# The last layer norm of a decoder step: bias and scaling moved from VectorE to TensorE and PSUM

## The reference, cut to what matters

```python
def layer_norm(x, g, b):
    mu = jnp.mean(xf, axis=-1, keepdims=True)
    var = jnp.mean(jnp.square(xf - mu), axis=-1, keepdims=True)
    y = (xf - mu) * lax.rsqrt(var + LN_EPS)
    return (y * g + b).astype(x.dtype)
...
x = layer_norm(ALPHA * x + moe_ffn(x, router_w, router_b, w_gate, w_up, w_down), ln2_g, ln2_b)
```

## Time and profile before

| | us |
|---|---|
| median of three executions | 1706.83 |
| the profiled execution, its whole time | 1705.88 |
| its span, first to last instruction | 1704.1 |
| TensorE busy | 1597.7 (94%) |
| VectorE busy | 687.1 (40%) |
| ScalarE busy | 382.9 (22%) |
| GpSimd busy | 43.4 (3%) |

### The profile page before, as it was taken

One profiled execution on the slowest core, in us unless ns is written; L12 is line 12 of the kernel. 1 busy time (PEld: TensorE's weight loads), 2 busy tenths in 40 slices (PEclk: granted clock), 3 DMA queues, 4 the chain that ended last, 5 costly groups with the idle time before them and its releaser, 6 DMA issues.

```text
span 1704.1 us, 23703 instructions
## 1 busy us (share of the span) xinstructions
PE 1597.7 (94%) x10374; PEld 1076.3 (63%) x10374; DVE 687.1 (40%) x991; ACT 382.9 (22%) x396; POOL 43.4 (3%) x79
## 2 busy tenths in 40 slices
PE   8999999999999999999999999898998988988995
PEld 8999999988999999983433432433334324324432
DVE  6546678647467565654620120200201101202706
ACT  5453555523344333240000000000000000000000
POOL 2000000012000000000000000000000000000000
PEclk9999999999999999999999999999999999999998
DMA  8675565579646759978999999999999999999996
GB/s 239 183 223 155 143 186 161 149 210 321 174 137 186 222 179 272 322 272 355 406 390 429 428 428 429 428 428 429 428 428 428 429 428 428 428 429 428 427 417 228
DMA packets 252719, 545.86 MB, mean 320 GB/s; under 512 B 6080, under 2 KB 219152, under 8 KB 228320
## 3 DMA queue, kind: packets, MB, share of 16 engines
q1 hardware_dynamic: 245888, 527.06, 82.0%
q0 software_dynamic: 4640, 15.47, 2.8%
q10 hardware_dynamic: 2112, 2.16, 0.4%
HBM read 537.73 MB, written 6.95 MB: 320 GB/s over the span
## 4 chain that ended last, share of the span: by engine, by line
PE 81%; DMA 13%; DVE 3%; ACT 2%; issue 1%; DVEq 0%; POOL 0%; ACTq 0%
PE bank L890 18%; PE bank L955 13%; PE bank L607 12%; PE bank L608 12%; PE bank L609 12%; DMA ring_high<-wu 9%; PE bank L865 5%; PE bank L1011 3%; PE bank L650 2%; DMA ring_high<-wd 2%; DMA ring_low<-w_in 1%; PE bank L976 1%; PE bank L945 1%; DMA ring_low<-wob 1%; ACT xt L1185 1%
## 5 line engine op out<-in xcount | busy, mean ns | idle before, releaser
L609 PE MATMUL bank<-x_hi,w_lo 128*128 128x264 f32 x1216 | 344.9, 284 | 0.0
L607 PE MATMUL bank<-x_hi,w_hi 128*128 128x264 f32 x1200 | 344.1, 287 | 0.0
L608 PE MATMUL bank<-x_lo,w_hi 128*128 128x264 f32 x1200 | 340.7, 284 | 0.0
L1226 DVE TENSOR_TENSOR w_lo<-ring_low,w_hi 128x2048 fp32r<-128x2048 f32 x107 | 245.1, 2291 | 146.6 <-ACT w_hi L1058 145.8
L890 PE MATMUL bank<-ring_low,reg_pk 128*64 128x512 f32 x1008 | 224.7, 595 | 21.1 <-DMA ring_low<-wu 18.6
L1058 ACT CAST w_hi<-ring_low 128x2048 fp32r<-128x2048 f32 x107 | 203.5, 1902 | 157.3 <-PE bank L609 90.0
L890 PE MATMUL bank<-ring_high,reg_pk 128*64 128x512 f32 x1024 | 225.1, 593 | 7.2 <-DMA ring_high<-wu 6.8
L609 PEld LDWEIGHTS bank<-x_hi,w_lo 128*128 128x128 f32 x1216 | 228.7, 188 | 0.0
L607 PEld LDWEIGHTS bank<-x_hi,w_hi 128*128 128x128 f32 x1200 | 226.8, 189 | 0.9 <-issue 0.8
L608 PEld LDWEIGHTS bank<-x_lo,w_hi 128*128 128x128 f32 x1200 | 227.0, 189 | 0.0
L890 PEld LDWEIGHTS bank<-ring_low,reg_pk 128*64 128x64 f32 x1008 | 69.7, 137 | 171.0 <-issue 132.1
(11 more groups left out here) (339 smaller groups left out, 1769.7 us busy)
## 6 DMA issues: line engine op xcount, KB each, us to landing
ring_low<-w_in SPq DMA_DIRECT2D x76, 1024.0 KB, 5.8
ring_high<-wg SPq DMA_DIRECT2D x34, 2048.0 KB, 23.8
ring_low<-wu SPq DMA_DIRECT2D x33, 2048.0 KB, 25.6
ring_high<-wd SPq DMA_DIRECT2D x32, 2048.0 KB, 27.5
ring_low<-wd SPq DMA_DIRECT2D x31, 2048.0 KB, 18.4
ring_low<-wg SPq DMA_DIRECT2D x30, 2048.0 KB, 33.6
ring_high<-wu SPq DMA_DIRECT2D x30, 2048.0 KB, 23.5
ring_low<-wo SPq DMA_DIRECT2D x16, 1024.0 KB, 6.5
```

What stands on the lines that cost most here:

```text
L607: pe.matmul(out, hi[k], of_hi[:, k, :], start=(k == 0), stop=False)
L608: pe.matmul(out, hi[k], of_lo[:, k, :], start=False, stop=False)
L609: mm = pe.matmul(out, lo[k], of_hi[:, k, :], start=False, stop=(k == kk - 1))
L1226: dve.tensor_tensor(lo_of(q), raw_of(q), hi_of(q).bitcast(F32), ALU.subtract).then_inc(lo_ready, 1)
```

## The change

- The two 1 MB broadcasts of gain and bias (`ln2p`) are gone. GpSimd loads instead 8 rows of 512 values (`ln2_rows`), a gain row and a bias row on partitions 32c and 32c + 1 for each column block.
- TensorE broadcasts the gain rows by four products (`gain_out`), placed in `down_last` behind the products of block 0. ScalarE copies the four banks to `ln2_gain` in SBUF.
- In `down_last` the scatter of block `c` - 1 moves from behind the products of block `c` to their middle, behind row group 3. The last unit is loaded in two halves, and TensorE waits for the second half before row group 4.
- Behind the last prompt add, TensorE broadcasts the bias rows into seven banks (`row_out`), the eighth when bank 0 has been read.
- For each piece VectorE runs only `centred`. TensorE multiplies the piece by a diagonal matrix of one over the standard deviation (`spread`) and accumulates onto the bias in PSUM (`y_part`). ScalarE makes the two diagonals and copies each bank out to `acc`, and SyncE writes it to the output.
- VectorE norms the sample tokens after the prompt pieces. ScalarE starts their four output transfers. TensorE's two small products for them stand behind pieces 3 and 5.

The diff, without the declarations and the overflow branch:

```diff
@@ sync
+                        if m < UNITS - 1:
+                            sp.dma_start(by_block(ring_slot(s)), src).then_inc(landed[s], 16)
+                        else:
+                            sp.dma_start(by_block(ring_slot(s))[:, 0:4, :], src[:, 0:4, :]).then_inc(landed[s], 16)
+                            sp.dma_start(by_block(ring_slot(s))[:, 4:8, :], src[:, 4:8, :]).then_inc(half_in, 16)
...
-            for a, par in enumerate((ln2g, ln2b)):
-                sp.dma_start(ln2p[:, a, :], par.partition_broadcast(P)).then_inc(ln2_in, 16)
...
+            for n in range(8):
+                tt, c = divmod(n, 4)
+                sp.wait_ge(y_ready, n + 1)
+                sp.dma_start(y[P * tt:P * tt + P, 512 * c:512 * c + 512], acc[:, tt, 512 * c:512 * c + 512]).then_inc(y_out, 16)
@@ gpsimd
+            pool.wait_ge(hid_ready, 2 * NPAIR - 1)
+            for c in range(4):
+                for a, par in enumerate((ln2g, ln2b)):
+                    pool.dma_start(ln2_rows[32 * c + a:32 * c + a + 1, :], par[512 * c:512 * c + 512].unsqueeze(0)).then_inc(rows_in, 16)
@@ tensor
+            def row_out(bank, c, a):
+                rows = slice(32 * c, 32 * c + 2)
+                return pe.matmul(bank[:, :], ident[rows, 32 * c + a:32 * c + a + 1].broadcast_to([2, P]), ln2_rows[rows, :], start=True, stop=(a == 0))
+            def gain_out():
+                for c in range(4):
+                    mm = row_out(psum[c], c, 0)
+                return mm
@@ down_last
                     for k in range(8):
+                        if c == 3 and k == 4:
+                            pe.wait_ge(half_in, 16)
                         for half in range(2):
                             mm = pe.matmul(...)
+                        if c and k == 3:
+                            scatter_last(i, c - 1)
                     mm.then_inc(w_used, 1)
-                    if c:
-                        scatter_last(i, c - 1)
+                    if c == 0:
+                        pe.wait_ge(rows_in, 16 * 8)
+                        gain_out().then_inc(gain_mm, 1)
@@ end of tensor
+            pe.wait_ge(gain_ev, 4)
+            pe.wait_ge(sc_ev, pairs * N_SC + (NPAIR * N_SC - 1))
+            for c in range(4):
+                row_out(psum[c], c, 1)
+            for c in range(3):
+                row_out(psum[5 + c], c, 1)
+            def y_part(n):
+                tt, c = divmod(n, 4)
+                bank = psum[n if n < 4 else n + 1 if n < 7 else 0]
+                if n == 0:
+                    pe.wait_ge(spread_ready, 1)
+                if n == 7:
+                    pe.wait_ge(y_ready, 1)
+                    row_out(bank, 3, 1)
+                pe.wait_ge(y_mul, n + 1)
+                pe.matmul(bank[:, :], spread[:, tt, :], acc[:, tt, 512 * c:512 * c + 512], start=False, stop=True).then_inc(y_mm, 1)
...
+            for n in range(4):
+                y_part(n)
+            sample_average(0)
+            for n in range(4, 6):
+                y_part(n)
+            sample_average(1)
+            for n in range(6, 8):
+                y_part(n)
@@ scalar
+                            if c == 0:
+                                act.wait_ge(gain_mm, 1)
+                                for q in range(4):
+                                    act.copy(ln2_gain[:, 512 * q:512 * q + 512], psum[q][:, :]).then_inc(gain_ev, 1)
...
+            act.wait_ge(l_inv, 2)
+            for tt in range(2):
+                ins = act.activation(spread[:, tt, :], ident[:, :], ACT.Identity, scale=mv[:, tt, 3:4])
+            ins.then_inc(spread_ready, 1)
...
+            for n in range(6):
+                y_done(n)
             act.wait_ge(l_var, 4)
             act.activation(mv[:, 2, 2:3], mv[:, 2, 1:2], ACT.Sqrt, bias=eps).then_inc(l_std, 1)
+            for n in range(6, 8):
+                y_done(n)
+            act.wait_ge(ys_ready, 1)
+            for nn in range(4):
+                act.dma_start(y[2 * P:2 * P + NS, 512 * nn:512 * nn + 512], acc_s[32 * nn:32 * nn + NS, :]).then_inc(y_out, 16)
@@ vector
             for tt in range(2):
                 dve.bn_aggr(mv[:, tt, 0:2], stat[:, tt, 0:4, :].rearrange("p n s -> p (n s)")).then_inc(l_var, 1)
+            dve.wait_ge(gain_ev, 4)
+            centred(0)
+            dve.wait_ge(l_std, 2)
+            dve.reciprocal(mv[:, 0:2, 3], mv[:, 0:2, 2]).then_inc(l_inv, 1)
+            centred(1)
             link(dve.bn_stats(stat[:, 2, 0, :], acc_s))
             dve.bn_aggr(ms[:, 0:2], stat[:, 2, 0, :]).then_inc(s_part, 1)
...
+            centred(2)
+            centred(3)
+            centred(4)
             dve.wait_ge(s_part, 1)
             dve.wait_ge(s_avg, 1)
...
             dve.tensor_tensor(ms[:, 1:2], ms[:, 1:2], ms[:, 2:3], ALU.add).then_inc(s_part, 1)
+            centred(5)
             dve.wait_ge(s_avg, 2)
             dve.tensor_copy(ms[:, 0:1], psum[4][:, 0:1])
             dve.tensor_copy(ms[:, 1:2], psum[4][:, 1:2]).then_inc(l_var, 1)
+            centred(6)
             dve.wait_ge(l_std, 3)
             link(dve.reciprocal(ms[:, 3:4], ms[:, 2:3]))
+            centred(7)
             dve.wait_ge(ln2q_in, 16 * 8)
...
```

More of the change, by code:

```diff
@@ L235, in build @@
         xg = reg_pk[:, 0:KD * P].rearrange("p (k s) -> p k s", s=P)
-        ln2p = low[:, 2, :].rearrange("p (a c) -> p a c", c=D)
+        ln2_gain = low[:, 2, 0:D]
+        ln2_rows = reg_pk[:, KD * P:KD * P + 512]
         ln2q = low[:, 3, 0:1024].rearrange("p (a c) -> p a c", c=512)
@@ L287, in build @@
         pick, _ = place("pick", [P, 3, 2, CAP])
+        spread = pick[:, 0:2, :, :].rearrange("p a b s -> p (a b s)").rearrange("p (t q) -> p t q", q=P)
         outer = pick[:, 0:2, :, :].rearrange("p a b s -> p (a b s)")
@@ L454, in _ @@
             with sp.If(pairs > 0):
+                sp.wait_ge(gain_ev, 4)
                 with sp.Fori(0, pairs) as j:
@@ L1035, in _, with sample_average @@
                     pair(j + NPAIR)
-            pe.wait_ge(quarter_ready, 1)
-            for n in range(2):
-                pe.wait_ge(s_part, n + 1)
-                pe.matmul(psum[n][:, 0:1], quarter, mv[:, 2, n:n + 1], start=True, stop=True).then_inc(s_avg, 1)
+                pe.wait_ge(sc_ev, pairs * N_SC + NPAIR * N_SC)
+                gain_out().then_inc(gain_mm2, 1)
+                pe.wait_ge(gain_ev2, 4)
+            pe.wait_ge(gain_ev, 4)
[14 more added lines that the diff above has]
+                pe.matmul(bank[:, :], spread[:, tt, :], acc[:, tt, 512 * c:512 * c + 512], start=False, stop=True).then_inc(y_mm, 1)
+            def sample_average(n):
+                pe.wait_ge(s_part, n + 1)
+                pe.matmul(psum[4][:, n:n + 1], quarter, mv[:, 2, n:n + 1], start=True, stop=True).then_inc(s_avg, 1)
+            pe.wait_ge(quarter_ready, 1)
+            for n in range(4):
[6 more added lines that the diff above has]
+                y_part(n)
         @block.scalar
@@ L1715, in _ @@
                 dve.wait_ge(again, 1)
+                dve.wait_ge(gain_ev2, 4)
             ms = mv[:, 2, :]
@@ L1719, in _, with centred @@
                 dve.bn_aggr(mv[:, tt, 0:2], stat[:, tt, 0:4, :].rearrange("p n s -> p (n s)")).then_inc(l_var, 1)
+            dve.wait_ge(gain_ev, 4)
+            def centred(n):
+                tt, c = divmod(n, 4)
+                cols = slice(512 * c, 512 * c + 512)
+                dve.scalar_tensor_tensor(out=acc[:, tt, cols], in0=acc[:, tt, cols], scalar=mv[:, tt, 0:1], in1=ln2_gain[:, cols],
+                                         op0=ALU.subtract, op1=ALU.mult).then_inc(y_mul, 1)
+            dve.wait_ge(l_var, 3)
+            centred(0)
+            dve.wait_ge(l_std, 2)
+            dve.reciprocal(mv[:, 0:2, 3], mv[:, 0:2, 2]).then_inc(l_inv, 1)
+            centred(1)
             dve.wait_ge(sc_ev, pairs * N_SC + NPAIR * N_SC)
@@ L1763, in _ @@
             dve.scalar_tensor_tensor(out=acc_s, in0=acc_s, scalar=ms[:, 3:4], in1=ln2q[:, 1, :], op0=ALU.mult, op1=ALU.add).then_inc(ys_ready, 1)
-            for n in range(5, 8):
-                centred(n)
-                scaled(n - 1)
-            scaled(7)
 def kernel(**inputs):
```

48 lines of the change are left out of this document (12 added, 36 removed).

## The result

The changed kernel took 1712.21 us in the median of six runs (1709.74 to 1715.35), the kernel before 1706.80 (1705.02 to 1708.11). The ratio is 1.0038 with a 95% interval of 1.0023 to 1.0053, so 3.9 to 9.0 us slower. The forecast was 1712.0. The time is right; of the terms it was made of, the one for the gain rows was 2.5 us too high and the one for the layer norm 1.4 us too low.

A forecast was written before the change was run, and what follows sets the result against it. The end was taken as TensorE until block 3 is scattered, then VectorE's adds, then the layer norm. Terms +2.7 + 1.2 + 0 + 1.5 = +5.4 us gave 1712.2 on the median, stated as 1712.0, range 1708.3 to 1714.8.

The forecast's parts named there:

- part 1: Gain rows in down_last: four row products, 3.44 us behind block 0, make everything behind later, +2.7 us (+2.5 to +3.1).
- part 2: Scatter in the block's middle: VectorE adds block c - 1 only after block c, +1.2 us (0 to +1.93).
- part 3: Split load of the last unit and missing broadcasts: 0, since TensorE reaches block 3 after the whole unit landed.
- part 4: Layer norm shared with TensorE: 18.6 us from L1719 to the end, before 17.1, so +1.5 us.
- the prediction's own signs: Wrong if row products pace under 0.7 us, block 1 starts before 1666, or pieces are late for VectorE, not TensorE.
- the third rival: TensorE's clock falls to 1.2 GHz in the layer norm through gaps of 1.0 and 0.4 us: about +13, 1725; chance 0.03.
- the second rival: Gain and bias rows of 2 partitions cost only 0.2 us, so the ends cancel: +0.2, median 1707.0; chance 0.14.
- The sign: Direction for the whole kernel: slower, chance 0.75, against 0.20 for no change and 0.05 for faster.

The follow-up runs named there:

- one row group: The changed kernel with all 8 gain and bias rows on partitions 0 and 1 instead of 32c and 32c + 1; ratio to the kernel before 1.0104.
- warm: The changed kernel with three full products of unused result added behind the sample scatter; ratio to the kernel before 1.0014.
- last unit whole: The changed kernel with the last unit loaded in one transfer as before; ratio to the kernel before 1.0039.
- and sample by SyncE: The changed kernel with scatter behind the block, three unused products, early averages, and sample tokens' transfers started by SyncE; ratio to the kernel before 1.0003.

## Why the prediction was right, and where it was not

The sum was +5.4; the tails show +4.35, and the medians +5.4 with an interval from +3.9. Step by step, in us after block 0's start:

| step | forecast | measured |
|---|---|---|
| block 1 starts (part 1) | +2.7 | 4.67 - 4.44 = +0.23 |
| norm start (part 2 on top) | +1.2 | 27.99 - 26.56 - 0.23 = +1.2 |
| split load (part 3) | 0 | without it, +0.7 more |
| norm start to the start of piece 0 | 3.8 | 3.2 |
| pieces 0 to 3 | 3.9 | 6.0 |
| end of piece 3 to the end | 11.0 | 10.8 |
| norm start to the end (part 4) | 18.6, +1.5 | 20.0, +2.9 |

**Part 1 failed in its size.** "Four row products, 3.44 us" is the step. The price of one was right; that they queue was wrong, and kernel "one row group" shows it: 3.69 on one group, 1.14 on four. The residual's products, which I took as the nearest row, lie four in a row on the partitions of one group, so they hardly could show it. The layout of the rows on partitions 32c, which stood in the diff, was the sign I passed over. The bias rows had the same error: 6.0 us forecast for seven, 1.99 measured at full clock ("warm"). By the prediction's own signs this step is refuted: the row products pace at 0.27 us (1.07 for four), under 0.7, and block 1 starts before 1666, if its time is counted from block 0 (1660.44 + 4.67 = 1665.11). In the trace's own time it starts at 1667.26, the layer norm at 1690.58, and both seem to meet the forecast (1667.6 and 1690.9), but only because this execution reached block 0 2.15 us later.

**Part 2 held**, mechanism and size: a 1.34 us wait for the adds of block 2, and +1.2 us, removed to 0.01 us by undoing it (26.78, against 26.56 + 0.23). Turning VectorE's order around removed 0.74 of it.

**Part 3 failed.** Its ground was that TensorE reaches block 3 at 1678.6. That rested on part 1's 2.7 us. With 0.23 in their place TensorE reaches it at 1676.2 in the time of the trace of before (15.76 us after block 0), half a microsecond after the unit's landing there, and where the unit came 1.1 us later, in "last unit whole", the half unit was worth 0.6 to 0.7.

**Part 4: the shape held, the cause of the loss was another.** As forecast, VectorE waited for the first average (4.32 us), TensorE waited 0.40 and 0.97 us in the two places named, and ScalarE issued the last transfers. But the forecast had the bias rows begin 0.05 us after the last prompt add; they began 2.6 us after it, in a standstill of TensorE that the forecast had put at nothing. And the forecast excluded the fall of the clock ("I count 2.4 GHz throughout", chance 0.03). It fell, for about 7 us, and cost 2.96 us of the tail by "warm". So what the third rival names was there, though ahead of the gaps that it gave as the reason; its price of +13 was not, because the clock came back after the first pieces. The cheap rows of the second rival were there as well, for a reason that the rival did not have.

Part 1 came out 2.5 us lower than forecast and part 4 1.4 higher, in which the clock's 3.0 and the standstill's 2.6 stand against the cheap bias rows. What is left, 1.1 us, is as much as the medians lie above the tails. With the clock at 1.00, as the forecast had it, the changed kernel's steps give 45.05 - 43.66 = +1.4 us in the tail ("warm"; its ratio of 1.0014 is +2.4 us) in place of +5.4. That the forecast came within 0.2 us of the median is luck.

The sign had a part that was right: from the norm start to the end it did not get shorter by moving half of VectorE's work (17.1 us before, 17.05 in "warm" at full clock, 20.0 in the changed kernel), because the work came back on TensorE with waits between three engines. With the clock at 1.00, the averages early, the sample tokens' transfers by SyncE and the scatter back in its place, the tail is 1.35 us shorter than before; the execution of "and sample by SyncE" shows that much and no more.

## What to carry to other kernels

Before pricing small products by their number, look at the partitions they lie on: on different groups of 32 they run beside one another, on one group they queue. A short stage on TensorE behind an idle stretch has to be priced at both clocks; filling the stretch with products shortened it here by 3 us, but did not hold the clock every time. When a step is moved ahead on one engine, look at what its consumer does first: the early scatter cost 1.2 us while VectorE's program had the copy-out first, and still 0.5 with the adds first (norm start 27.25 against 26.78). And give a match in absolute time no weight before the start of the stage has been taken off on both sides.

## What the runs showed of the hardware

- Four float32 products of 2 x 128 by 512 took 1.14 us on four partition groups and 3.69 us on one.
- Between the last product ahead of the jump over the overflow branch and the first behind it TensorE stood still for 1.7 to 2.7 us in the eight profiles where nothing filled it; the engine's waits in that stretch name VectorE, but three more products fitted in and moved the bias rows by 0.2 us only.
- The granted clock fell to 0.50 after this standstill although the bias rows (2 partitions) and full products followed at once, and it was back some 3.4 to 10.2 us later. In one execution it was at 0.50 from 1669 to 1671 us although TensorE was busy all the time ("one row group"). The same TensorE program kept 1.00 in one execution and lost it in another. What decides it was not settled.
- Full products of 128 x 128 by 512 with a semaphore wait each came at 0.86 us (3.67 for four), where the scatters' 0.965 had been the nearest row.
- From the last piece's product to the end of the span it took 5.01 to 5.10 us with four 16 KB transfers issued by ScalarE behind the last copy, and 4.50 and 4.55 with them issued by SyncE ahead of the last prompt piece.
